# A decoder step with a mixture of experts on one core: loads around the first gather, counts inside the last product, products of the identity in waits

## What is computed

```python
x = x + g1 * mix                                   # mix ends with m @ w_o
h = rmsnorm(x, norm2) * (1 + sc2) + sh2
glog = h @ w_rg + b_rg;  gtop, gsel = top_k(glog, 1)          # 4 groups
elog = (h @ w_re + b_re) of the chosen group;  top_k(elog, 2) # 8 experts each
out = sum over chosen experts of weight * (silu(h @ w_e_gate) * (h @ w_e_up)) @ w_e_down
x = x + g2 * out;  y = rmsnorm(x, final_norm)
```

## Time and profile before

| | before |
|---|---|
| median of 3 runs | 1186.23 us (1186.14 to 1190.28) |
| the profiled execution | 1186.55 us |
| its span | 1184.9 us |
| mean granted TensorE clock | 0.955 of full |
| TensorE busy | 1074.9 us (91%) |
| VectorE busy | 567.7 us (48%) |
| ScalarE busy | 252.1 us (21%) |
| GpSimd busy | 154.6 us (13%) |
| moved by DMA | 226.34 MB, 191 GB/s over the span |

### The profile page before, as it was taken

How to read it: one execution, slowest core, us unless ns; L and a number is a source line. 1 busy time by engine, 2 the same in 40 slices (tenths; PEclk the granted TensorE clock), 3 DMA queues, 4 the chain that set the end, 5 groups by cost and what they waited for, 6 DMA issues and landing times.

```text
span 1184.9 us, 15164 instructions
## 1 busy us (share of the span) xinstructions
PE 1074.9 (91%) x5901; PEld 704.2 (59%) x5901; DVE 567.7 (48%) x1158; ACT 252.1 (21%) x677; POOL 154.6 (13%) x307
## 2 busy tenths in 40 slices
PE   5999998999999999899999999998948988987776
PEld 3445777777777887887577777754534322332222
DVE  3123737477787494576764556434564201210127
ACT  3100010567622222464111010101111000100011
POOL 3000500012304000051100000100011111111101
PEclk8999998999999999899999999998968989998898
DMA  9995543242414443125462422459174999999975
GB/s 333 337 260 183 186 77 74 48 128 69 76 41 72 107 82 70 37 73 161 123 226 79 114 68 75 146 130 310 76 277 194 416 421 415 418 419 420 412 299 185
DMA packets 96854, 226.34 MB, mean 191 GB/s; under 512 B 21422, under 2 KB 40167, under 8 KB 84082
## 3 DMA queue, kind: packets, MB, share of 16 engines
q1 hardware_dynamic: 86998, 202.70, 52.3%
q10 hardware_dynamic: 4660, 12.75, 3.2%
q0 software_dynamic: 5120, 9.88, 2.4%
HBM read 210.60 MB, written 23.08 MB: 197 GB/s over the span
## 4 chain that ended last, share of the span: by engine, by line
PE 27%; SPq 12%; DMA 7%; DVE 3%; issue 1%; ACTq 0%; ACT 0%; POOL 0%; DVEq 0%
PE ps L2265 16%; SPq L2953 7%; DMA w_gate_up<-w_e_up 4%; PE ps L2771 3%; SPq L2967 3%; PE ps L2295 3%; DMA mod_new<-mod_scratch 2%; SPq L2945 2%; PE ps L2788 1%; PE ps L3060 1%; DMA x_gathered<-h_scratch,toks 1%; PE ps L2332 1%; PE ps L3063 0%; PE ps L2759 0%; PE ps L2797 0%
## 5 line engine op out<-in xcount | busy, mean ns | idle before, releaser
L2771 PE MATMUL ps<-w_gate_up,xT 128*64 128x512 f32 x528 | 132.9, 643 | 26.5 <-DMA w_gate_up<-w_e_up 26.5
L2771 PEld LDWEIGHTS ps<-w_gate_up,xT 128*64 128x64 f32 x528 | 41.0, 147 | 115.8 <-issue 79.6
L695 PE MATMUL ps<-hT,w_ring 128*128 128x288 f32 x384 | 97.6, 415 | 3.7 <-PEq L105 3.7
L2925 DVE TENSOR_TENSOR act<-silu_gate,ps 128x256 f32<-128x256 f32 x17 | 7.2, 421 | 195.1 <-ACT silu_gate L2741 195.1
L695 PEld LDWEIGHTS ps<-hT,w_ring 128*128 128x128 f32 x384 | 73.8, 194 | 24.1 <-issue 4.0
L2788 PE MATMUL ps<-w_down,actT 128*64 128x512 f32 x264 | 62.1, 598 | 8.8 <-DVE actT L2929 8.8
L1345 PE MATMUL ps<-hT,w_ring 128*128 128x288 f32 x264 | 67.7, 406 | 0.0
L1630 DVE SCALAR_TENSOR_TENSOR conv_y<-z_staged,convT,conv_y 128x600 f32<-128x600 f32 x72 | 59.7, 842 | 9.4 <-ACT conv_y L1080 7.6
L1345 PEld LDWEIGHTS ps<-hT,w_ring 128*128 128x128 f32 x264 | 49.3, 190 | 13.2 <-issue 0.5
L2697 POOL DMA_INDIRECT pair_scratch<-y_block,pairs x16 | 16.1, 1005 | 210.2 <-ACT y_block L2749 210.2
L2788 PEld LDWEIGHTS ps<-w_down,actT 128*64 128x64 f32 x264 | 18.0, 136 | 41.2 <-issue 29.2
(11 more groups left out here) (581 smaller groups left out, 2010.5 us busy)
## 6 DMA issues: line engine op xcount, KB each, us to landing
w_down<-w_e_down SPq DMA_DIRECT2D x32, 1024.0 KB, 26.1
w_ring<-w_in SPq DMA_DIRECT2D x15, 2048.0 KB, 13.9
w_gate_up<-w_e_gate SPq DMA_DIRECT2D x30, 1024.0 KB
w_gate_up<-w_e_up SPq DMA_DIRECT2D x30, 1024.0 KB
w_ada_slots<-w_ada SPq DMA_DIRECT2D x8, 2048.0 KB, 8.8
w_ada_slots<-w_ada SPq DMA_DIRECT2D x4, 1024.0 KB, 14.9
w_ring<-w_pa SPq DMA_DIRECT2D x2, 2048.0 KB, 7.7
w_ring<-w_pb SPq DMA_DIRECT2D x2, 2048.0 KB, 7.9
```

Of the source, the lines that this page charges most:

```text
L695: last = nc.tensor.matmul(psum[:, bank + hf, 0:HALF], w[:, c, 128 * q:128 * q + 128], x[:, c, HALF * hf:HALF * hf + HALF], start=c == 0, s ...
L2771: last = te.matmul(psum[side(u), s % 2, :], xT[:, s % 2, c, side(u)], gu[s % GU_BUFS][:, u, :, c, :], start=c == 0, stop=c == KC - 1)
```

## The change

- TensorE: `early_counts` stands between the two halves of the last o-projection product and no longer behind it. 12 products of the identity with itself (`spare_products`) stand before `late_counts`, 14 behind the late table; they write a part of PSUM that nobody reads.
- GpSimd: for the last tile, one step multiplies and adds where there were two.
- ScalarE: stores the last x2 tile, which SyncE did.
- SyncE: the first half of w_gate_up 2 is loaded behind w_down 1, the second half and the first half of w_down 3 once the first gather has landed. The wait for `constd` and the second half of w_down 3 move into step 1 of the loop, behind the gate/up loads of step 4.
- VectorE: `over_blocks` moves behind the first evacuation; `count_u` gets another place, since its old one is under the evacuated rows.

```diff
--- before.py
+++ after.py
@@ -1973,7 +1973,8 @@
         self.parts = work("pair_parts", [128, 2, 2, NT, NE // 2], BF16)
         assert work.offset <= m.merge_base + 59392
         work = Region(nc, m.merge_base + 59392)
-        self.onehot_step, self.count = work("onehot_step", [128, 2, NT, NE // 2], BF16), work("count_u", [128, NE], U32)
+        self.onehot_step = work("onehot_step", [128, 2, NT, NE // 2], BF16)
+        self.count = Region(nc, m.spare[1] + 4096)("count_u", [128, NE], U32)
         self.step, self.chosen, self.counted, self.hot, self.tabled = (sem(n) for n in (
             "r_dve", "r_chosen", "r_counted", "r_onehot", "r_tabled"))
         self.split = sem("r_parts")
@@ -2125,12 +2126,12 @@
         sp.wait_ge(mev, mev_after(PAIRS - 1))
         load_down(sp, m, ins, 0, (0, 1))
         load_gate_up(sp, m, ins, 1, (2, 3))
-        for p, t in enumerate(ORDER):
+        for p, t in enumerate(ORDER[:END]):
             sp.wait_ge(x2d, 2 * p + 2)
             sp.dma_start(m.x2_dram[tile_cols(t), :], m.x2[0:ROWS[t], t, :]).then_inc(x2st, 16)
-            if p == NT - 2:
-                sp.wait_ge(omm, 10)
-                load_down(sp, m, ins, 1, (2, 3))
+        sp.wait_ge(omm, 10)
+        load_down(sp, m, ins, 1, (2, 3))
+        load_gate_up_of(sp, m, ins, 2, 0, 4)
         sp.wait_ge(xwd, 2)
         sp.wait_ge(xsq, NT + 1)
         sp.wait_ge(x2st, 16 * NT)
@@ -2140,7 +2141,6 @@
         sp.wait_ge(x4tr, 2)
         sp.wait_ge(h2st[0], 48)
         sp.wait_ge(h2st[1], 32)
-        load_gate_up(sp, m, ins, 2, (4, 5))
 
     def gpsimd(pool):
         p = nc.gpsimd
@@ -2167,10 +2167,8 @@
             pool.wait_ge(rsd, 2 * t + 1)
             if t == END:
                 pool.wait_ge(xsq, NT + 1)
-                p.tensor_scalar(ss[:, NT:NT + 1], ss[:, NT:NT + 1], 1.0 / D, None, ALU.mult).then_inc(rsd, 1)
+                p.tensor_scalar(q, ss[:, NT:NT + 1], 1.0 / D, q, ALU.mult, ALU.add).then_inc(rsd, 1)
                 pool.wait_ge(rsd, 2 * t + 2)
-                p.tensor_tensor(q, q, ss[:, NT:NT + 1], ALU.add).then_inc(rsd, 1)
-                pool.wait_ge(rsd, 2 * t + 3)
             p.tensor_tensor(q, q, m.half[:, 0:1], ALU.pow).then_inc(rsd, 1)
 
     def scalar(act):
@@ -2248,6 +2246,7 @@
         square_half(0)
         keep_half(0)
         square_half(1)
+        act.dma_start(m.x2_dram[tile_cols(ORDER[END]), :], m.x2[:, ORDER[END], :]).then_inc(x2st, 16)
         keep_half(1)
         store_h2(END)
 
@@ -2374,6 +2373,11 @@
             if hi == NT:
                 last.then_inc(r.tabled, 1)
 
+        def spare_products(n):
+            pe.wait_ge(ld, END)
+            for _ in range(n):
+                te.matmul(psum[:, 7, 0:128], m.ident[:, :], m.ident[:, :], start=True, stop=True)
+
         whole = range(KC)
         o_half(0, 0, whole)
         o_half(0, 1, whole)
@@ -2390,15 +2394,18 @@
                 constant_logits()
             o_half(p, 1, range(0, 4))
             logits(p - 1)
+            if p == END:
+                early_counts()
             o_half(p, 1, range(4, KC))
-        early_counts()
         last_transposes(0)
         logits(END, range(0, 4))
         table(0, EARLY_POS)
         last_transposes(1)
         logits(END, range(4, KC))
+        spare_products(12)
         late_counts()
         table(EARLY_POS, NT)
+        spare_products(14)
 
     def vector(dve):
         v = nc.vector
@@ -2542,7 +2549,7 @@
         slot_rows_of(nc, dve, m, r, 0, EARLY_POS, psum[:, 2, 0:96])
         residual(END, 1)
         scaled(1)
-        dve.wait_ge(rsd, 2 * END + 4)
+        dve.wait_ge(rsd, 2 * END + 3)
         dve.wait_ge(x4tr, 2)
         h = h2[:, END % 2, :]
         v.scalar_tensor_tensor(h, h, rstd[:, END:], modp[:, 1, :], ALU.mult, ALU.add).then_inc(h2d, 1)
@@ -2655,9 +2662,9 @@
             eng.nop()
 
     def sync(sp):
+        sp.wait_ge(gth[0], 16)
+        load_gate_up_of(sp, m, ins, 2, 1, 5)
         load_down_of(sp, m, ins, 3, 0, 6)
-        sp.wait_ge(constd, 1)
-        load_down_of(sp, m, ins, 3, 1, 7)
 
         def experts(s):
             pair = block_pair(s)
@@ -2673,6 +2680,9 @@
                 if max(lo, GU_BUFS) <= g < hi:
                     sp.wait_ge(gmm, s + 1)
                     load_gate_up(sp, m, ins, g, experts(g))
+                if s == 1:
+                    sp.wait_ge(constd, 1)
+                    load_down_of(sp, m, ins, 3, 1, 7)
                 if max(lo, WD_BUFS) <= d < hi:
                     sp.wait_ge(dmm, s + 1)
                     load_down(sp, m, ins, d, experts(d))
@@ -2908,10 +2918,10 @@
 
         def run(lo, hi):
             if lo == 0:
-                over_blocks()
                 weights()
             x_evacuate(lo)
             if lo == 0:
+                over_blocks()
                 over_counts()
                 over_pairs()
             for s in range(lo, hi):
@@ -2951,6 +2961,12 @@
             for h in range(parts):
                 cs = slice(KC // parts * h, KC // parts * (h + 1))
                 sp.dma_start(m.gu[s % GU_BUFS][:, u, k, cs], w[e][:, cs]).then_inc(m.gu_loaded[s % GU_BUFS], 16)
+
+
+def load_gate_up_of(sp, m, ins, s, u, e):
+    for k, name in enumerate(("w_e_gate", "w_e_up")):
+        w = ins[name][0].rearrange("g e (p c) f -> (g e) p c f", p=128)
+        sp.dma_start(m.gu[s % GU_BUFS][:, u, k], w[e]).then_inc(m.gu_loaded[s % GU_BUFS], 16)
 
 
 def load_down_of(sp, m, ins, s, u, e):
```

## The result

The changed kernel took 1178.93 us (median of 6 runs, 1175.39 to 1181.51) beside 1186.41 for the kernel before: ratio 0.9929, 95% interval 0.9905 to 0.9954. Run again beside the experiments it took 1175.61, ratio 0.9904 (0.9888 to 0.9921). The profiled execution took 1179.83, its span is 1178.1. The forecast was 1173.2.

The account below looks back on a forecast made before the run. Bound: one unbroken stream of expert weight loads. Block 0's product ends at 904.4 - 4.3 (gather) - 0.8 (clock) = 899.3; the stream starts there, not at 912.7: 1186.55 - 13.4 = 1173.2 us. Range 1170.0 to 1179.0.

Parts of the forecast that it names:

- rival B: Last x2 and h2 stores starve beside 4 MB of loads, gather issued as late as before: 1177.4 to 1178.2, chance 0.18.
- What bounds the kernel: Expert stage: one unbroken stream of weight loads binds; the end moves with its start, if the queue never runs dry.
- The wait: SyncE's loop: constants' wait moved behind block 4's loads, over before it is reached; block 3's loads start 8.3 us earlier.
- Early counts and chain: Last o-projection to token table: VectorE takes the residual 1.6 us earlier; first gather issued at 880.1, not 881.97.
- The gather: First gather, fewer loads ahead: takes 6.8 us, not 9.26, and lands 4.3 us earlier, 1.9 of them from earlier issue.
- The clock: TensorE around the first gather: identity products raise the granted clock for transposes and slot rows; 0.8 us, bounds 0 and 2.3.
- Rival A: Identity products hold TensorE's full clock through the gather: 1.5 us more gain, 1171.7, chance 0.2.
- From stream to end: Expert loads to kernel end: the 13.4 us earlier start of block 3's loads passes whole into the time.
- C: SyncE's loop: loads come to wait for buffers, a hole in each of 14 steps; slower, 1192.5, chance 0.04.
- D: Only the wait's move counts, the gather's chain comes out slower by a few microseconds: gain about 5 us, 1181.5, chance 0.06.
- The gate/up waits: TensorE's waits for gate/up weights: a total not falling from 26.5 toward 18 us would show the forecast wrong.

Follow-up runs that it names:

- wait_only: Kernel before with only the wait for the routing constants and the second half of w_down 3 moved behind step 4's gate/up loads: 1178.16 us, ratio 0.9925.
- half_behind: Changed kernel with the first half of w_gate_up 2 loaded behind the first gather instead of ahead of it: 1176.59 us, ratio 0.9924.
- early_down: Changed kernel with w_down 1 loaded after the ninth half of the o-projection, not the tenth: 1172.38 us, ratio 0.9875.
- no_spares: Changed kernel without its 26 products of the identity: 1177.45 us, ratio 0.9931.
- before_again: Kernel before, unchanged, run once more for a second trace: 1186.21 us.
- after_again: Changed kernel, unchanged, run once more beside the experiments: 1175.61 us, ratio 0.9904.

## Why the prediction was right or wrong

The direction was right: 0.7% faster, 0.5 to 1.0% by the interval. 1178.93 lies in the range of 1170.0 to 1179.0, but only 0.07 us inside it, nearer to rival B (1177.4 to 1178.2, chance 0.18) than to the forecast of 1173.2. With runs from 1175.39 to 1181.51 that is partly luck. The gain was 7.5 us (10.9 by the second series) where the sum had 13.4. By its steps:

- **What bounds the kernel**: right. The DMA engines are full from the stream's start to the last load, and wait_only moved one wait and got 8.3 us (8.9 by the ratio) where 8.3 were expected.
- **The wait**: right. The constants' signal came before it was asked for; the half of w_down 3 was issued 0.5 us after the load ahead of it (917.11 and 917.61).
- **Early counts and chain**: right. Table at 125.4 in place of 127.1, 1.7 us of the 1.9 forecast (the second trace of before has 125.6, so part of that is how the first one fell). The mechanism shows within each trace: in both traces of before VectorE took the residual 2.6 us after the last product had ended, in both of after 0.03 us after it; less the 0.9 us by which the ten counts lengthen the product, that is the 1.6 forecast.
- **The gather**: the step that failed. It took 6.42 us (6.8 forecast), but was issued 0.5 us later and not 1.9 earlier, and landed 2.3 us earlier and not 4.3. The sum had let both last stores pass for nothing: I counted their bytes among the 7.3 MB in front and left their landing out of the chain, though I had named it as rival B. B's mechanism is what happened: h2 store 10.67 us against 3.5 before, gather held until 884.05. B let all of the 4.3 us go, with the stream at 903.6 to 904.4; the trace has it at 903.20, which is 901.6 counted as in before. So what it cost is the 2.4 us by which the gather left later than forecast, and half_behind and early_down show it from the other side. In the time the price can't be told from what was measured: 1178.93 and 1175.61 lie on both sides of B's.
- **The clock**: 0.8 us taken, 0.5 seen against the first trace, and no_spares has the same without the products. So no run shows a gain from this term in the changed kernel. (Against it the prediction had one more sign than it used: the stretch at 1050 in the earlier trace rows is at 1.00 with TensorE busy 7.64 of 10 us, so not every long stretch at 1.00 is one without gaps.) The products' own cost was also mispriced: a product of the identity shows as two matmuls in the trace (x24 for 12), so 12 took 5.12 us and not 3.0; they end at 878.49, just when the late counts could start (878.46). Another microsecond of them would have delayed the table. Rival A, the clock held through the gather, did not happen here; in half_behind and early_down it did.
- **From stream to end**: the sum passed the stream's start through unchanged. Of 11.4 us at the stream (158.5 to 147.1; 11.0 counted from the half of w_down 3, as the sum does) 10.0 were left at the last load and 8.4 at the end. The second part is the final stage, 65.4 us from last load to end against 63.7, which before_again shows as scatter (64.8). Where the first 1.0 to 1.4 us went I can't say; the second trace of before has 8.9 at the stream and 8.4 at the last load.
- **The basis**: the sum was made against one trace, whose stream started 2.5 us later than in the other. Of these 2.5 us, 1.5 were left at the last load and 0.6 at the end, so they explain a part of the distance of 5.7 us between forecast and result, how much stays open. It could not be seen from one profile; the range had no term for it.
- **C and D**: no ten microseconds between 920 and 1110 have a DMA share under 1.00, so buffers did not bind. D neither: the chain came out 2.3 us faster and not slower. The gate/up waits fell to 22.6 (22.0 in after_again) and not to 18: TensorE gained less on the stream than thought. By its own words the prediction took such a total for a sign of being wrong; it fell half the way.

## What to carry to other kernels

Where a queue of loads is the bound, look for the in-order wait that keeps it empty, and price the move by the hole in the DMA share: by the medians that held within a microsecond. When loads are pulled forward, list every small store that a later step waits for and give each the time that it takes beside those loads, 6.4 to 10.8 us here for half a megabyte; freeing an earlier moment for the load (early_down) was worth more than moving it behind the wait. And count milestones from a common instruction ahead of the change before comparing two traces. Where TensorE stands idle and the profile names no releaser, look at its sequencer before filling the gap: the 11 products put there only delayed the branch.

## What the runs showed of the hardware that I had not expected

- The last h2 store, 0.5 MB, landed in 3.5 us in before, where the loads beside it had been issued 7 us earlier and the DMA share was 0.89 falling to 0.48. Beside 4 MB of loads issued 3.3 to 4.6 us before it, it took 9.9 to 10.8 us, beside 2 MB 6.4 to 7.6 (8.7 where they were issued 0.1 to 0.5 us before it). The x2 store took 10.1 us from ScalarE's queue and 10.6 from SyncE's.
- Behind the last down product TensorE stood idle 3.5 to 4.2 us, and 4.8 us counted from the end of work put into that gap. It is the rest of a branch that took 5.9 to 6.8 us on TensorE and 0.05 to 0.08 us on the other engines.
- The granted clock in the first products of the final stage fell in 12 of 14 traces and stayed in two whose gap was 3.5 us; gaps 0.2 us longer and more went with 1.5 to 3 us more for eight products.
- The same code ahead of the change lay up to 6.4 us apart from execution to execution (749.79 to 756.14), a good part of the scatter of the runs (8 to 9 us between the fastest and slowest of some kernels, 1168.60 to 1177.76 for early_down).
